# Two attention layers: low halves of late output-weight pieces moved on VectorE and ScalarE, one value projection moved between the first scores

## The chip, the cores and the metric

The kernel runs on one core of a Trainium2 chip. The metric is the device time of one execution in microseconds (us); the time quoted is the median of three runs. TensorE, VectorE, ScalarE, GpSimd and SyncE are written PE, DVE, ACT, POOL and SP, as in the rows of the profile. Each engine works through its own instructions in program order and waits on semaphores for the others.

## The reference, cut to what matters

Two blocks follow each other on x [1, 512, 1024], in float32. The first has two layers, each an attention, a layer norm with the residual, a mixture of 32 experts (two per token) and another layer norm. Its first attention is windowed with sinks, its second has low-rank (latent) queries, keys and values. The second block (convolutions, stick-breaking attention, retention, feed-forward) is not touched by the change.

```python
def swa_sink_gqa(x, w_in, sinks, w_o):      # layer 0
    ...
    m = jnp.maximum(jnp.max(sc, -1, keepdims=True), sink)
    e = jnp.exp(sc - m)
    p = e / (jnp.sum(e, -1, keepdims=True) + jnp.exp(sink - m))
    o = jnp.einsum('bnhgqk,bnkhd->bnqhgd', p.astype(vb.dtype), vb)
    return o.reshape(b, s, qd) @ w_o

def mla(x, w_down, q_norm, kv_norm, w_uq, w_ukv, w_o):   # layer 1
    ...
    kv = (ckv @ w_ukv).reshape(b, s, B_HEADS, B_NOPE + B_V)
    ...
    o = causal_attention(q, k, kv[..., B_NOPE:], (B_NOPE + B_ROPE) ** -0.5)
    return o.reshape(b, s, B_HEADS * B_V) @ w_o

for i in range(DEPTH):
    h = layer_norm(alpha * h + y, ...)       # y: the attention
    y = hier_moe(h, ...)
    h = layer_norm(alpha * h + y, ...)
```

## The kernel before, in words

The order of each engine's instructions is written out by hand, one Python function per engine (`_(pe)`, `_(act)`, `_(dve)`, `_(sp)`), in `window_layer` (first layer) and `latent_layer` (second).

**Split products.** A dense float32 product is three PE matmuls: both factors are split into a high part (ACT copies it to a rounded type) and a low part (DVE subtracts the high part), and `split_matmul` (L232 to L234) adds high by high, low by high and high by low. Weights come in pieces of 128x2048: SP loads a piece into one of two raw buffers (`load`), ACT makes the high part (`high(p)`, semaphore `hi_made`), DVE the low part (`low(p)`, `lo_made`). The output weight has four pieces, O to O+3. In `window_layer` these are pieces 6 to 9, written in the traces as win_w or win_w_o; in `latent_layer` pieces 8 to 11, written lat_w_o.

**Units.** The attention works on 16 units u, four heads by a tile n of 128 queries. For each unit PE makes `scores(u)`; DVE takes row maxima (`maxes(u)`: a reduction from PSUM and one to three tiny instructions); ACT takes exponentials (`exps(u)`); DVE divides (`norms(u)`: a reciprocal and four multiplications); PE transposes the probabilities (`turn(u)`); ACT copies them (`keep_turned(u)`); PE multiplies by the values (`mix(u)`); ACT and DVE make the high and low part of the result (`out_high(u)`, `out_low(u)`). Parts of the output projection (`out_part`) of a finished query tile stand between turn and mix of later units, so that PE has work while the other engines do the next softmax.

**First layer, where the change is.** Units 0, 2, 4 and 6 belong to query tile 0, so `out_part(0, 0)` comes with u = 7. PE's order there is mix(6), turn(7), scores(9), out_part(0,0), mix(7), turn(8), scores(10), out_part(0,1), mix(8). ACT's is exps(7), keep_turned(6), out_high(6), high(O+3), exps(8), keep_turned(7), out_high(7). DVE's is maxes(6), maxes(7), norms(6), out_low(5), maxes(8), low(O+2), norms(7), out_low(6), maxes(9), low(O+3), norms(8). The scores banks alternate, so scores(u) waits for exps(u-2). `out_part(0, 0)` needs pieces O and O+1, `out_part(0, 1)` needs O+2 and O+3.

**Second layer.** All scores share four banks: `scores(u)` waits for exps(u-1). Before scores(0) PE has made the value projections ("v", 0) and ("v", 1); the other six `up_unit(UP[("v", m)])` come two per unit, in PSUM bank 7 one after the other, each waiting for ACT's `keep_up` of the one before. ("v", 2) and ("v", 3) stood with u = 0, after turn(0). ACT's high(10) stood before out_high(2), high(11) before out_high(3); DVE's low(10) stood before norms(3), low(11) before norms(4). From u = 4 on out_part(0, ...) runs.

**After an attention.** SP loads expert weights into three sets. Those loads wait for points of the attention (`lo_made` complete, `scored`, `mixed`, `am.out_made`), later ones for blocks of experts that PE has used up. Routing and the experts follow, then the next layer.

Of the kernel before, what the change touches and what calls it, by code (L numbers as in the profile page):

```python
# [14 lines left out]
F32, BF16, I32, U32 = mybir.dt.float32, mybir.dt.bfloat16, mybir.dt.int32, mybir.dt.uint32  # L15
F32R = mybir.dt.float32r
ALU = mybir.AluOpType
# [548 lines left out]
def window_layer(k, base, layer, r, weights):  # L566
# [6 lines left out]
    raw = plan.put("raw", 80, [P, 2, 2048])  # L573
# [15 lines left out]
    K, V, Q, O = 0, 1, 2, 6  # L589
# [15 lines left out]
    with k.nc.Block(no_gpsimd_drain=True) as block:  # L605
# [380 lines left out]
        def _(dve):  # L986
# [6 lines left out]
            def low(p):  # L993
                dve.wait_ge(hi_made, p + 1)
                hi, lo = pieces[p]
                dve.tensor_tensor(laid(p, lo[:, :]), as_read(p), laid(p, hi[:, :].bitcast(F32)), ALU.subtract).then_inc(lo_made, 1)

            def rope(q):
                dve.wait_ge(bare_kept, q + 1)
                rope_tile(k, dve, link, bare[:, q % 2, :], k.ps[:, 6 if q < 2 else 3, :], tables, tmp, (rotated, q + 1))  # L1000
                dst = kT[:, q, :] if q < 2 else qT[:, q - 2, :]
                dve.tensor_tensor(dst, tmp[:, 0, :], tmp[:, 1, :], ALU.add).then_inc(placed, 1)
                dve.wait_ge(placed, q + 1)

            def maxes(u):
                n, gp, half = units[u]
                w, b = width(n), u % 2
                mine = sinks[:, 8 * gp:8 * gp + 8].rearrange("p (g a) -> p g a", g=2)[:, :, 2 * half:2 * half + 2]
                four = lambda y: y[:, b, :].rearrange("p (g i) -> p g i", g=2)
                dve.wait_ge(scored, u + 1)  # L1010
                link(dve.tensor_reduce(mx[:, b, :], heads(u)[:, :, 0:w], AX.X, ALU.max))
                link(dve.scalar_tensor_tensor(four(mx), four(mx), HD ** -0.5, mine, ALU.mult, ALU.max))
                link(dve.tensor_scalar(nm[:, b, :], mx[:, b, :], -1.0, None, ALU.mult))
                dve.tensor_tensor(four(es), mine, four(nm), ALU.add).then_inc(maxed, 1)
# [64 lines left out]
            norms(5)  # L1079
            out_low(4)  # L1080
            maxes(6)
            maxes(7)
            norms(6)
            out_low(5)
            maxes(8)
            low(O + 2)
            norms(7)
            out_low(6)
            maxes(9)
            low(O + 3)  # L1090
            for u in range(8, len(units)):
                norms(u)
                if u in (9, 11, 13, 15):
                    am.add(k, dve, (u - 9) // 4, (u - 9) // 2 % 2, 7)
                out_low(u - 1)
                if u + 2 < len(units):
                    maxes(u + 2)
                if u == 12:
                    am.norm(k, dve, 0)
# [307 lines left out]
def latent_layer(k, base, layer, cl, r, weights):  # L1407
# [80 lines left out]
    with k.nc.Block(no_gpsimd_drain=True) as block:  # L1488
# [64 lines left out]
        def _(pe):  # L1553
# [151 lines left out]
            for i in range(6, UP[("v", 2)]):  # L1705
                up_unit(i)
            scores(0)
            for u in range(len(units)):
                n, g = units[u]
                if u + 1 < len(units):  # L1710
                    scores(u + 1)
                turn(u, 0)
                if u < 3:
                    up_unit(UP[("v", 2 * u + 2)])
                if u >= 4:
                    out_part((u - 4) // 4, 2 * (u % 4))
                if n >= 2:
                    turn(u, 1)
                if u < 3:
                    up_unit(UP[("v", 2 * u + 3)])  # L1720
                if u >= 4:
                    out_part((u - 4) // 4, 2 * (u % 4) + 1)
                mix(u)
# [15 lines left out]
        def _(act):  # L1739
# [119 lines left out]
            for i in range(6, UP[("v", 2)]):  # L1859
# [3 lines left out]
                if i == 17:  # L1863
                    high(9)
            exps(0)
            for u in range(len(units)):
                keep_turned(u)
                if u < 3:
                    keep_up(UP[("v", 2 * u + 2)])
                if u + 1 < len(units):  # L1870
                    exps(u + 1)
                if u < 3:
                    keep_up(UP[("v", 2 * u + 3)])
                if u == 2:
                    high(10)
                if u == 3:
                    high(11)
                if u in (9, 13):
                    am.root(act, (u - 9) // 4)
                out_high(u)  # L1880
            copy = lambda dst, src: act.activation(dst, src, ACT.Copy)
            for half in range(2):
                take_turned(k, copy, act, rt, 0, half)
# [10 lines left out]
        def _(dve):  # L1894
# [106 lines left out]
            for u in range(len(units)):  # L2001
                if u + 1 < len(units):
                    maxes(u + 1)
                if u == 2:
                    low(10)
                if u == 3:
                    low(11)
                if u in (10, 14):
                    am.norm(k, dve, (u - 10) // 4)
                if u + 1 < len(units):  # L2010
                    norms(u + 1)
                if u >= 4 and u % 2 == 1:
                    am.add(k, dve, (u - 4) // 4, (u // 2) % 2, 7)
                out_low(u)
            am.norm(k, dve, 2)
            for half in range(2):
                am.add(k, dve, 3, half, out_bank(3, half))
# [1099 lines left out]
```

## Time and profile before

| what | value |
|---|---|
| median of 3 runs | 2742.12 us |
| lowest and highest | 2739.75, 2742.32 us |
| profiled execution, its own time | 2739.88 us |
| its span | 2738.1 us |
| mean granted clock of PE | 0.970 of full speed |
| PE busy | 2515.5 us, 92% of the span |
| DVE busy | 1074.0 us, 39% |
| ACT busy | 753.9 us, 28% |

Times in rows are counted from the span's start. The first attention takes the time up to about 232, its experts the time to about 720; the second attention ends at about 1015 and its experts at about 1500; the rest is the second block. A timeline row gives start, duration, engine, line, operation, output and inputs, shapes and count, and in brackets how long the engine was idle just before and what released it. PE matmuls are pipelined, so durations of neighbours overlap: starts are what to read.

### The profile page before, as it was taken

To read this page: it belongs to the slowest core of one execution; us is meant where nothing else is said; L and a number is where in the kernel's file an instruction comes from. 1 tells how busy PE (TensorE), PEld (TensorE's weight loads), DVE (VectorE), ACT (ScalarE), POOL (GpSimd) and SP (SyncE) were. 2 spreads that over 40 slices of the span, in tenths; PEclk is the share of its full clock that TensorE was granted. 3 is DMA by queue.
4 is the path that set the end of the run, shared out by engine and by line. 5 is a ranking of instruction groups with operands and counts; after the bars stand their busy time and mean duration, and the time that the engine had idled before them with its cause. 6 is when DMAs were issued, how large, how long until landed. Compare 5 with 4: busy or idle time off the path is not lost.

```text
span 2738.1 us, 36816 instructions
## 1 busy us (share of the span) xinstructions
PE 2515.5 (92%) x14582; PEld 1856.1 (68%) x14582; DVE 1074.0 (39%) x1594; ACT 753.9 (28%) x1217; POOL 182.2 (7%) x302
## 2 busy tenths in 40 slices
PE   8897999877898979998888899999999999999998
PEld 7575665444476666664544677888887877888887
DVE  4653111010354551110100666656542566556542
ACT  3530000000245420000001353543332354433331
POOL 0001111111000001111111000000000010000000
PEclk9998999999998989999999999999999999999999
DMA  6238999999722079999998412222333212223231
GB/s 169 69 139 352 406 407 406 411 406 406 282 93 78 9 297 402 404 406 411 409 411 350 173 62 93 77 93 93 107 124 108 70 62 93 78 93 108 93 123 54
DMA packets 174825, 576.56 MB, mean 211 GB/s; under 512 B 20496, under 2 KB 104016, under 8 KB 125042
## 3 DMA queue, kind: packets, MB, share of 16 engines
q1 hardware_dynamic: 164146, 558.07, 53.8%
q0 software_dynamic: 10560, 16.81, 1.9%
q8 instruction: 86, 1.41, 0.2%
q14 instruction: 33, 0.27, 0.0%
HBM read 569.56 MB, written 23.07 MB: 216 GB/s over the span
## 4 chain that ended last, share of the span: by engine, by line
PE 66%; SPq 20%; DMA 5%; DVE 4%; issue 3%; ACT 2%; POOLq 0%; DVEq 0%; POOL 0%; ACTq 0%
PE ps L232 15%; PE ps L233 15%; PE ps L234 15%; SPq L1151 13%; SPq L1157 7%; PE ps L1301 6%; PE ps L1319 4%; DMA first_weights<-in_moe_w_up 2%; PE ps L1271 1%; ACT lat_probs L1808 1%; PE ps L1634 1%; PE ps L1618 1%; PE ps L2300 1%; PE ps L2336 1%; DMA r_x<-resid 1%
## 5 line engine op out<-in xcount | busy, mean ns | idle before, releaser
L232 PE MATMUL ps<-l_h_hi,l_w_hi 128*128 128x512 f32 x896 | 353.0, 394 | 0.0
L1301 PE MATMUL ps<-first_weights,moe_xsT 128*64 128x256 f32 x2688 | 310.9, 381 | 44.5 <-DMA first_weights<-in_moe_w_up 28.0
L234 PE MATMUL ps<-l_h_hi,l_w_lo 128*128 128x512 f32 x896 | 348.8, 389 | 0.0
L233 PE MATMUL ps<-l_h_lo,l_w_hi 128*128 128x512 f32 x896 | 348.8, 389 | 0.0
L1380 DVE TENSOR_TENSOR moe_hid<-moe_silu,ps 128x256 f32<-128x256 f32 x64 | 27.0, 422 | 779.8 <-PE ps L1301 779.8
L1301 PEld LDWEIGHTS ps<-first_weights,moe_xsT 128*64 128x64 f32 x2688 | 224.1, 137 | 141.0 <-issue 90.7
L2830 DVE TENSOR_TENSOR l_w_lo<-l_raw,l_w_hi 128x2048 fp32r<-128x2048 f32 x76 | 174.1, 2293 | 270.2 <-ACT l_w_hi L2591 270.2
L1353 ACT ACTIVATE moe_ys<-ps 128x512 f32<-128x512 f32 x64 | 38.2, 597 | 685.7 <-PE ps L1319 685.7
L1319 PE MATMUL ps<-first_weights,moe_hidT 128*64 128x512 f32 x672 | 180.6, 685 | 38.5 <-DVE moe_hidT L1382 38.5
L2591 ACT ACTIVATE l_w_hi<-l_raw 128x2048 fp32r<-128x2048 f32 x76 | 145.6, 1918 | 179.5 <-PE ps L234 168.7
L232 PEld LDWEIGHTS ps<-l_h_hi,l_w_hi 128*128 128x128 f32 x896 | 168.2, 188 | 37.7 <-issue 2.9
L233 PEld LDWEIGHTS ps<-l_h_lo,l_w_hi 128*128 128x128 f32 x896 | 168.3, 188 | 35.5 <-issue 1.4
L234 PEld LDWEIGHTS ps<-l_h_hi,l_w_lo 128*128 128x128 f32 x896 | 168.2, 188 | 35.2
L1301 PE MATMUL ps<-first_ring,moe_xsT 128*64 128x256 f32 x1344 | 157.3, 384 | 25.5 <-DMA first_ring<-in_moe_w_up 14.8
L1301 PEld LDWEIGHTS ps<-first_ring,moe_xsT 128*64 128x64 f32 x1344 | 113.1, 138 | 72.8 <-issue 47.4
L1319 PEld LDWEIGHTS ps<-first_weights,moe_hidT 128*64 128x64 f32 x672 | 61.1, 154 | 129.1 <-issue 129.1
L1319 PE MATMUL ps<-first_ring,moe_hidT 128*64 128x512 f32 x352 | 88.8, 649 | 20.1 <-DVE moe_hidT L1382 20.1
L1259 POOL DMA_INDIRECT r_y<-moe_ys,moe_put x64 | 65.6, 1025 | 300.5 <-ACT moe_ys L1353 285.7
L1350 ACT ACTIVATE moe_silu<-ps 128x256 f32<-128x256 f32 x64 | 24.6, 384 | 215.7 <-PE ps L1301 215.7
L2873 DVE SCALAR_TENSOR_TENSOR l_gate<-l_glu,l_par,l_gate 128x512 f32<-128x512 f32 x120 | 81.8, 751 | 0.1
L232 PE MATMUL ps<-l_w_hi,l_act_hi 128*128 128x512 f32 x192 | 75.4, 393 | 0.0
L234 PE MATMUL ps<-l_w_hi,l_act_lo 128*128 128x512 f32 x192 | 75.0, 390 | 0.0
(577 smaller groups left out, 4314.6 us busy)
## 6 DMA issues: line engine op xcount, KB each, us to landing
first_weights<-in_moe_w_up SPq DMA_DIRECT2D x84, 1024.0 KB
first_weights<-in_moe_w_down SPq DMA_DIRECT2D x84, 1024.0 KB
first_weights<-in_moe_w_gate SPq DMA_DIRECT2D x84, 1024.0 KB
first_ring<-in_moe_w_up SPq DMA_DIRECT2D x44, 1024.0 KB
first_ring<-in_moe_w_down SPq DMA_DIRECT2D x44, 1024.0 KB
l_raw<-in_ffn_up SPq DMA_DIRECT2D x44, 1024.0 KB, 5.1
first_ring<-in_moe_w_gate SPq DMA_DIRECT2D x40, 1024.0 KB
l_raw<-in_w_in SPq DMA_DIRECT2D x22, 1024.0 KB, 5.1
```

The costliest lines, as they stand in the source:

```text
L232: pe.matmul(out, stationary[0], moving[0], start=first, stop=False)
L233: pe.matmul(out, stationary[0], moving[1], start=False, stop=False)
L234: return pe.matmul(out, stationary[1], moving[0], start=False, stop=last)
L1151: sp.dma_start(self.gate_up[s][m][:, 4 * c:4 * c + 4, :].rearrange("p j c -> p (j c)"), a[name][layer, e, c * 512:(c + 1) * 512, :].rearra ...
L1157: sp.dma_start(self.down[s][:, 2 * c:2 * c + 2, :].rearrange("p j c -> p (j c)"), a["moe_w_down"][layer, e, c * 256:(c + 1) * 256, :].rear ...
L1259: pool.indirect_dma_start(out=r.y_dram, out_offset=bass.IndirectOffsetOnAxis(ap=put[:, 0:1], axis=0), in_=ys[:, :], in_offset=None, bounds ...
L1301: ins = pe.matmul(k.ps[64 * h:64 * h + 64, 2 + m, 0:256], xsT[:, j, :], piece[:, j % 4, 256 * h:256 * h + 256], start=j == 0, stop=j == ND ...
L1319: ins = pe.matmul(k.ps[64 * h:64 * h + 64, 4, :], hidT[:, j % 2, 64 * (j // 2):64 * (j // 2) + 64], weights.down[s][:, j, 512 * h:512 * h ...
L1353: act.activation(ys[:, :], k.ps[:, 4, :], ACT.Copy).then_inc(ys_kept, 1)
L2591: act.activation(ring[n][0], piece(m), ACT.Copy).then_inc(hi_made, 1)
L2830: dve.tensor_tensor(lo, piece(m), hi.bitcast(F32), ALU.subtract).then_inc(lo_made, 1)
L2873: ins = dve.scalar_tensor_tensor(acc, glu[:, i, c:c + SEQ], par[:, l, 2, 2 * c + i:2 * c + i + 1], acc, ALU.mult, ALU.add)
```

## The change

In `window_layer` DVE makes the low parts of pieces O+2 and O+3 in two halves of 1024 columns each (`low_half`). The halves of O+2 stand before maxes(7) and before norms(7), and norms(7) now comes before maxes(8). The halves of O+3 stand before maxes(9) and behind norms(8). In `latent_layer` the value projection ("v", 2) moves on PE from behind turn(0) to between scores(0) and scores(1), and its copy on ACT to behind exps(0); high(10) and high(11) move behind out_high(2) and out_high(3), low(10) and low(11) from before norms(3) and norms(4) to behind out_low(2) and out_low(3).

```diff
@@ window_layer, DVE
+            def low_half(p, half):
+                dve.wait_ge(hi_made, p + 1)
+                hi, lo = pieces[p]
+                part = slice(1024 * half, 1024 * half + 1024)
+                return dve.tensor_tensor(lo[:, part], raw[:, p % 2, part], hi[:, part].bitcast(F32), ALU.subtract)
...
             out_low(4)
             maxes(6)
+            low_half(O + 2, 0)
             maxes(7)
             norms(6)
             out_low(5)
+            low_half(O + 2, 1).then_inc(lo_made, 1)
+            norms(7)
             maxes(8)
-            low(O + 2)
-            norms(7)
             out_low(6)
+            low_half(O + 3, 0)
             maxes(9)
-            low(O + 3)
             for u in range(8, len(units)):
                 norms(u)
+                if u == 8:
+                    low_half(O + 3, 1).then_inc(lo_made, 1)
...
@@ latent_layer, PE
             scores(0)
+            up_unit(UP[("v", 2)])
             for u in range(len(units)):
...
                 turn(u, 0)
-                if u < 3:
+                if 0 < u < 3:
                     up_unit(UP[("v", 2 * u + 2)])
@@ latent_layer, ACT
             exps(0)
+            keep_up(UP[("v", 2)])
             for u in range(len(units)):
                 keep_turned(u)
-                if u < 3:
+                if 0 < u < 3:
                     keep_up(UP[("v", 2 * u + 2)])
                 if u + 1 < len(units):
                     exps(u + 1)
                 if u < 3:
                     keep_up(UP[("v", 2 * u + 3)])
-                if u == 2:
-                    high(10)
-                if u == 3:
-                    high(11)
                 if u in (9, 13):
                     am.root(act, (u - 9) // 4)
                 out_high(u)
+                if u in (2, 3):
+                    high(8 + u)
@@ latent_layer, DVE
                 if u + 1 < len(units):
                     maxes(u + 1)
-                if u == 2:
-                    low(10)
-                if u == 3:
-                    low(11)
...
                     norms(u + 1)
...
                 out_low(u)
+                if u in (2, 3):
+                    low(8 + u)
```

**DVE in the first layer, from behind maxes(8) to norms(7), before.** The 128x2048 row is low(O+2); the three rows behind it are norms(7).

```order
L1013 TENSOR_SCALAR win_nm<-win_mx 128x4
L1014 TENSOR_TENSOR win_es<-win_sinks,win_nm 128x4
L996 TENSOR_TENSOR win_w_o_lo<-win_raw,win_w_o_hi 128x2048
L1019 TENSOR_TENSOR win_rd<-win_sm,win_es 128x4
L1020 RECIPROCAL win_rd<-win_rd 128x4
L1022 TENSOR_SCALAR win_probs<-win_probs,win_rd 128x256 x4
```

The same place now, from out_low(5) on. Lines are those of the changed file.

```order
L1034 TENSOR_TENSOR win_o_lo<-ps,win_o_hi 128x256
L1002 TENSOR_TENSOR win_w_o_lo<-win_raw,win_w_o_hi 128x1024
L1025 TENSOR_TENSOR win_rd<-win_sm,win_es 128x4
L1026 RECIPROCAL win_rd<-win_rd 128x4
L1028 TENSOR_SCALAR win_probs<-win_probs,win_rd 128x256 x4
L1017 TENSOR_REDUCE win_mx<-ps 128x4
L1018 SCALAR_TENSOR_TENSOR win_mx<-win_mx,win_sinks 128x4
L1019 TENSOR_SCALAR win_nm<-win_mx 128x4
L1020 TENSOR_TENSOR win_es<-win_sinks,win_nm 128x4
```

Only half a piece stands ahead of norms(7) now, and maxes(8), with its reduction L1017, has moved behind norms(7).

**DVE in the second layer, u = 2, before.** The first two rows are maxes(3), the 128x2048 row is low(10), then come norms(3), out_low(2) and the reduction of maxes(4).

```order
L1944 TENSOR_REDUCE lat_nm<-ps 128x4
L1945 TENSOR_SCALAR lat_nm<-lat_nm 128x4
L1912 TENSOR_TENSOR lat_w_o_lo<-lat_raw,lat_w_o_hi 128x2048
L1950 RECIPROCAL lat_rd<-lat_sm 128x4
L1952 TENSOR_SCALAR lat_probs<-lat_probs,lat_rd 128x128 x4
L1959 TENSOR_TENSOR lat_o_lo<-ps,lat_o_hi 128x2x128
L1944 TENSOR_REDUCE lat_nm<-ps 128x4
```

And now:

```order
L1953 TENSOR_REDUCE lat_nm<-ps 128x4
L1954 TENSOR_SCALAR lat_nm<-lat_nm 128x4
L1959 RECIPROCAL lat_rd<-lat_sm 128x4
L1961 TENSOR_SCALAR lat_probs<-lat_probs,lat_rd 128x128 x4
L1968 TENSOR_TENSOR lat_o_lo<-ps,lat_o_hi 128x2x128
L1921 TENSOR_TENSOR lat_w_o_lo<-lat_raw,lat_w_o_hi 128x2048
L1953 TENSOR_REDUCE lat_nm<-ps 128x4
```

low(10) has left its place ahead of norms(3) for one directly ahead of maxes(4).

**PE in the second layer, from scores(0) to turn(0), now.** The first three rows are scores(0), the six L232 to L234 rows are ("v", 2), then come scores(1) and turn(0).

```order
L1627 MATMUL ps<-lat_k,lat_q 128x128 x4
L1630 MATMUL ps<-lat_kr,lat_qr 128x128 x4
L1632 MATMUL ps<-maskab,identb 128x128 x4
L232 MATMUL ps<-lat_uv_hi,lat_c_kv_hi 128x512
L233 MATMUL ps<-lat_uv_lo,lat_c_kv_hi 128x512
L234 MATMUL ps<-lat_uv_hi,lat_c_kv_lo 128x512
L232 MATMUL ps<-lat_uv_hi,lat_c_kv_hi 128x512
L233 MATMUL ps<-lat_uv_lo,lat_c_kv_hi 128x512
L234 MATMUL ps<-lat_uv_hi,lat_c_kv_lo 128x512
L1627 MATMUL ps<-lat_k,lat_q 128x128 x4
L1630 MATMUL ps<-lat_kr,lat_qr 128x128 x4
L1632 MATMUL ps<-maskab,identb 128x128 x4
```

Before, scores(1) followed scores(0) directly, and the six projection matmuls stood behind turn(0).

## Rows read from the trace of the kernel before

**Rows 1.** The page: chain that ended last, shares of the span by engine.
```profile
PE 66%; SPq 20%; DMA 5%; DVE 4%; issue 3%; ACT 2%; POOLq 0%; DVEq 0%; POOL 0%; ACTq 0%
```
**Rows 2.** Waits of PE, 106 to 137 us: us in total, times, longest.
```profile
PE ps L747 <- DVE win_probs L1022: 7.6, 4, 4.7
```
**Rows 3.** Timeline of PE, first layer: start, us, instructions [idle before, releaser].
```profile
118.58 0.65 PE L759 MATMUL ps<-win_probsT,win_v 128*64 128x256 f32 x4 [0.19 <-ACT win_probsT L907]
123.98 1.97 PE L747 MATMUL ps<-cst,win_probs 128*128 128x128 f32 x8 [4.75 <-DVE win_probs L1022]
...
128.73 0.50 PE L232 MATMUL ps<-win_w_hi,win_o_hi 128*128 128x512 f32 x1
...
131.70 1.08 PE L759 MATMUL ps<-win_probsT,win_v 128*64 128x256 f32 x8
134.40 1.09 PE L747 MATMUL ps<-cst,win_probs 128*128 128x128 f32 x8 [1.61 <-DVE win_probs L1022]
...
136.91 0.50 PE L232 MATMUL ps<-win_w_o_hi,win_o_hi 128*128 128x512 f32 x1
```
**Rows 4.** Timeline of DVE, same stretch.
```profile
113.17 1.23 DVE L1011 TENSOR_REDUCE win_mx<-ps 128x4 f32<-128x1024 f32 x1 [1.16 <-PE ps L734]
...
118.44 1.23 DVE L1011 TENSOR_REDUCE win_mx<-ps 128x4 f32<-128x1024 f32 x1 [1.86 <-PE ps L734]
...
120.18 2.29 DVE L996 TENSOR_TENSOR win_w_o_lo<-win_raw,win_w_o_hi 128x2048 fp32r<-128x2048 f32 x1
...
122.79 1.14 DVE L1022 TENSOR_SCALAR win_probs<-win_probs,win_rd 128x256 f32<-128x256 f32 x4
...
130.59 2.28 DVE L996 TENSOR_TENSOR win_w_lo<-win_raw,win_w_hi 128x2048 fp32r<-128x2048 f32 x1
```
**Rows 5.** Timeline of ACT, same stretch: end of exps(7), and high(O+3).
```profile
117.82 0.22 ACT L898 ACTIVATION_READ_ACCUMULATOR win_probs<-ps,win_nm 128x1 f32 x1
...
119.56 1.90 ACT L879 ACTIVATE win_w_hi<-win_raw 128x2048 fp32r<-128x2048 f32 x1
```
**Rows 6.** Instructions on win_raw: duration ns min/median/max, first and last start.
```profile
L1034 DVE TENSOR_TENSOR win_w_lo<-win_raw,win_w_hi x1: 1216/1216/1216, 11.1 to 11.1; 128x1024 fp32r<-128x1024 f32 x1
```
**Rows 7.** Windows: PE, PEld, DVE, ACT, POOL busy (count), PE clock, DMA share, GB/s.
```profile
119.20:124.00 4.80, 0.05 (x3) 0.02 (x1) 4.63 (x12) 4.10 (x11) 0.00 (x0) 0.77 0.00 0
124.00:128.70 4.70, 4.70 (x18) 3.02 (x18) 0.26 (x1) 1.02 (x1) 0.00 (x0) 0.50 0.02 3
```
**Rows 8.** Timeline of PE, second layer: the first row of scores or turn.
```profile
833.92 0.71 PE L1618 MATMUL ps<-lat_k,lat_q 64*128 64x128 f32 x8 [0.78 <-ACT lat_v L1800]
...
837.92 0.71 PE L1618 MATMUL ps<-lat_k,lat_q 64*128 64x128 f32 x8 [2.53 <-ACT lat_probs L1808]
...
845.65 0.71 PE L1618 MATMUL ps<-lat_k,lat_q 64*128 64x128 f32 x8
...
863.26 1.12 PE L1634 MATMUL ps<-cst,lat_probs 128*128 128x128 f32 x4 [3.19 <-DVE lat_probs L1952]
...
866.90 2.08 PE L1618 MATMUL ps<-lat_k,lat_q 64*128 64x256 f32 x8 [0.71 <-ACT lat_probs L1808]
...
872.29 1.97 PE L1634 MATMUL ps<-cst,lat_probs 128*128 128x128 f32 x8 [1.61 <-DVE lat_probs L1952]
```
**Rows 9.** Timeline of ACT, second layer: high(10).
```profile
857.99 1.90 ACT L1763 ACTIVATE lat_w_o_hi<-lat_raw 128x2048 fp32r<-128x2048 f32 x1
```
**Rows 10.** Timeline of DVE, second layer: the reduction of maxes(4).
```profile
863.46 1.22 DVE L1944 TENSOR_REDUCE lat_nm<-ps 128x4 f32<-128x1024 f32 x1
```
**Rows 11.** Windows of the second layer, columns as in rows 7.
```profile
837.90:842.10 4.20, 4.18 (x28) 3.54 (x29) 1.92 (x7) 0.60 (x1) 0.00 (x0) 0.59 0.00 0
...
875.80:878.90 3.10, 3.10 (x25) 2.28 (x23) 1.32 (x5) 1.34 (x6) 0.00 (x0) 0.94 0.62 262
```
**Rows 12.** Timeline of SP: first expert weights behind the last output part, first layer.
```profile
209.59 0.80 SPq L1151 DMA_DIRECT2D first_ring<-in_moe_w_gate  x2
```
**Rows 13.** A window of the first experts, columns as in rows 7.
```profile
300.00:400.00 100.00, 93.62 (x666) 61.02 (x662) 10.11 (x21) 7.25 (x15) 16.68 (x28) 0.95 1.02 406
```

## The prediction

> **What bounds the kernel now.** I read the chain of work that ended last first: PE holds 66% of it and the DMA queue of SP 20% [rows 1]. So there are two kinds of stretches: the attentions and the second block, where PE sets the pace, and the experts, where the weight stream does: 406 GB/s with the DMA engines full, while PE waits in between [rows 13]. The edits lie in the attentions only. The second view is PE's waits there: between 106 and 137 us PE waits 7.6 us for normalised probabilities, 4.7 of them at one place [rows 2]. The third is the timeline of PE, DVE and ACT around such a wait, to see what stood ahead of the late work. The fourth is the granted clock of the same stretches.
>
> **First layer, what is late.** mix(6) starts at 118.58 and lasts 0.65, then PE has nothing until turn(7) at 123.98 [rows 3]. turn(7) needs norms(7), which ends at 122.79 + 1.14 = 123.93 [rows 4]. Its input, exps(7), was done at 118.04 [rows 5]. Between the two DVE did maxes(8), 118.44 to 120.26, and then the whole of low(O+2), 2.29 us [rows 4]. The gap is not all: PE is granted 0.50 (1.2 GHz) from 124.0 to 128.7, straight behind it, though it works without a pause there, and 0.77 over the gap itself [rows 7].
>
> **First layer, step by step.** A half piece costs 1.22 us (a row of this very form exists) against 2.29 for the whole [rows 4, 6], so each split adds 2 x 1.22 - 2.29 = 0.15 us to DVE. The first half of O+2 lies in the idle 1.16 us before maxes(7), the second in the idle 1.86 us before maxes(8) [rows 4]; cost on the path 0.05 at most. If that cover were gone each would cost its 1.22. norms(7) takes 1.55 us (122.38 to 123.93). It now starts at 118.1 and ends at 119.65, so turn(7) starts at 119.7. turn and scores of a wide unit take 136.91 - 134.40 = 2.51 us at full clock: out_part(0,0) starts at 122.2. What it needs is there: maxes(8) now 119.6 to 121.4, out_low(6) to 121.7. out_part takes 131.70 - 128.73 = 2.97: mix(7) starts at 125.2, takes about 1.0 to the next start, turn(8) could start at 126.2. Does norms(8) come in time? high(O+3) ends at 121.46 [rows 5], so the first half of O+3 runs 121.7 to 122.9, maxes(9) to 124.6, norms(8) to 126.15. That is a tie. The second half of O+3 ends at 127.3, and out_part(0,1), its only reader, starts at 126.2 + 2.5 = 128.7. Before, low(O+3), from 130.59, held norms(8) and turn(8) until 134.40 [rows 3, 4]. **The term is 134.40 - 126.2 = 8.2 us.** Its ends: if a half piece does come in front of norms(8), 7.0; with the tie won, 8.4. I take 8.2, the sum of rows. It holds only with the clock at full speed, which I expect since the gap that came before the fall shrinks from 4.75 to 0.5 us.
>
> The Trainium skill, page "VectorE: DVE Perf Modes", section on the TRN2 errata, speaks against the halves: operands in SBUF pay a fixed extra latency in every instruction, so work should not be cut small. The trace agrees, at 0.15 us per cut; by that rule alone the change would cost 0.3 us on an engine that idles beside it.
>
> **Second layer, first scores.** scores(0) starts at 833.92 and scores(1) at 837.92, since scores, maxes, exps and the next scores form one chain of 4.0 us in which PE idles 2.53 [rows 8]. ("v", 2) is six matmuls of some 0.39 us or less; it fits in the idle time, and ACT's copy of it comes behind exps(0), where ACT would wait for turn(0). Then the same chain of 4.0 us links scores(1) and scores(2), plus 0.1 for keep_turned(0) ahead of exps(1): scores(2) at 842.0 against 845.65 [rows 8]. PE's own work in that time (turn(0), ("v", 3), mix(0)) just fits. **This term is 3.65 us.** It includes that the granted clock, 0.59 between 837.9 and 842.1 [rows 11], stays up, because the idle before it shrinks from 2.53 to about 1. If it does not, the term is 3.1. Units 1 and 2 keep their pace, which ACT's copies set.
>
> **Second layer, pieces 10 and 11.** I count in times of before, to be shifted by 3.65. scores(4) ends at 863.26 - 3.19 = 860.07; turn(3) then waited 3.19 us for norms(3), which stood behind low(10) [rows 8]. Now norms(3) is done by 858.3 and turn(3) and mix(3) run at once. What is late next: out_high(2) goes first on ACT, high(10) runs 858.4 to 860.3 instead of from 857.99 [rows 9], low(10) with its 2.29 to 862.6, and behind it is maxes(4), which starts at 862.6 instead of 863.46 [rows 10]. From maxes(4) to scores(5) it is 866.90 - 863.46 = 3.44. So scores(5) starts at 866.05, only 0.85 earlier: the wait for norms(3) has largely become one, of about 4.2 us, for maxes(4). From scores(5) to turn(4) it was 5.39 with 1.61 of waiting for norms(4), behind low(11). low(11) now runs behind out_low(3), so 5.39 - 1.61 = 3.78: turn(4) at 869.83 against 872.29, 2.46 earlier. Then the clock: PE now works without a pause from 866.05. In the first layer it was back at full speed after 4.7 us of that [rows 7], which would be 870.8 here; before, it came back near 875.8, and the part between turn(4) and mix(4) ran slow [rows 11]. That gives about 1.1 more. **This term is 3.6 us.** Ends: 2.46 if all stays at half clock as before; 5.0 if the clock never falls, where maxes(5), behind low(11), becomes the limit. I take the value between, by the row of the first layer.
>
> The Trainium skill, page "TensorE: Matmul & The Clock Gate", section on HAM oscillation, says that gaps between groups of matmuls put the array back to 1.2 GHz, so that a gap costs more than itself. That speaks against the new 4.2 us gap. By it the 5.0 us end of the last term is out of reach and the rest of the sum stands; the trace agrees [rows 8, 11], with 0.59 behind an idle of 2.53 us.
>
> **Does it reach the end?** After both places PE has no other long wait, and every transfer of expert weights waits for a point of the attention: the six of the first ring are issued at 209.59, behind the last output part [rows 12]. The stream at 406 GB/s starts from there and moves with it, unless it has a start that the attention doesn't set. I charge nothing for it.
>
> **The sum.** 8.2 + 3.65 + 3.6 = 15.45. The profiled execution took 2739.88 us for a span of 2738.1: 2724.4 for it. It is 2.2 us below the median of the runs, 2742.12, from which it is 2726.7. I predict **2726 us**.
>
> **Rivals.**
> (a) One gain is lost: the tie at norms(8) and the order behind it fail, or the gap at scores(5) grows and eats the second layer's terms. For it: both margins are under 0.2 us. Against: then other work moves earlier too. Time 2742.1 less 8.2 or less 7.3: 2734 to 2735, and anything between there and the forecast.
> (b) The expert stage swallows the gains: it is bound by its weight stream [rows 13], and if the stream's start were not tied to the attention, PE would only wait longer for weights. For it: SP's 20% of the chain. Against: the issue at 209.59. Time 2742.
> (c) Slower. The new gap of 4.2 us at scores(5) drops the clock, and it stays at 1.2 GHz through the dense part behind, where each us of work takes two. The sum has it back at full speed by 870.8. To lose the 15.4 us and 5.5 more, at half a us lost for each us run slowly, the slow stretch would have to go on for another 42 us, to about 913; from there on this case decides. For it: the gap is longer than any before it in this layer. Against: 4.7 us of steady work brought the clock back in the first layer. Time then 2748.
> (d) That the halves don't do what they say is excluded: the order of DVE shows them.
>
> **The chances.** A difference of 0.2%, 5.5 us, is about what a measurement of this kernel can tell from none. Forecast 0.77; (a) 0.14, still faster; (b) 0.06; (c) 0.03. So faster 0.91, same 0.06, slower 0.03. Bounds of the terms: 7.0 + 3.1 + 2.5 = 12.6 and 8.4 + 3.7 + 5.0 = 17.1, from either of 2739.9 and 2742.1: 2722.8 to 2729.5. With run-to-run spread and the nearer half of (a) the range is 2721 to 2732.
>
> **What would show it.** In the changed profile: turn(7) of the first layer with idle of 0.5 us or less before it, clock 1.00 from 120 to 129, out_part(0,1) near 128.7; in the second layer the 2.53 us idle before scores(1) down to about 1, and one idle of about 4.2 us before scores(5) with 1.2 GHz behind it for some 5 us. The experts must take as long as before, 8 us earlier in the first layer and 15 in the second. The prediction is wrong if norms(8) comes later than mix(7), or if the experts' stretch grows by what the attention gave.

## The result and the profile after

| what | before | changed |
|---|---|---|
| median of 5 runs on one chip | 2739.79 us | 2721.77 us |
| lowest and highest | 2737.54, 2742.32 us | 2719.08, 2726.82 us |
| profiled execution, its own time | 2739.88 us | 2721.77 us |
| its span | 2738.1 us | 2719.9 us |
| mean granted clock of PE | 0.970 | 0.976 |
| PE busy | 2515.5 us, 92% | 2500.8 us, 92% |

The ratio is 0.9931, 95% interval 0.9919 to 0.9942: 16 to 22 us faster. Run again beside the experiments, the same kernel gave 0.9941 (0.9928 to 0.9955). The forecast was 2726 us, with a gain of 15.45 us.

The first view is the chain of work that ended last, which answers to [rows 1]. Its shares add up to only 45% of the span: this time the chain goes back no further than 1493 us, the end of the second experts, so it doesn't tell how much the experts' weight stream holds.

```profile
PE 41%; DVE 2%; ACT 1%; DMA 1%; issue 0%; SPq 0%; DVEq 0%; ACTq 0%
```

The second is the list of PE's waits from 98 to 130 us, which now takes in turn(5) to turn(8), as [rows 2] did up to 137. The columns are the sum in us, the number of waits and the longest.

```profile
PE ps L747 <- DVE win_probs L1028: 3.1, 3, 2.1
```

7.6 us of waiting for normalised probabilities have become 3.1, and the longest, 4.7, is 2.1. The timeline of PE in the first layer answers to [rows 3]: start, duration, instructions, and in brackets the idle time before.

```profile
110.36 1.70 PE L747 MATMUL ps<-cst,win_probs 128*128 128x128 f32 x8 [0.73 <-DVE win_probs L1028]
...
117.70 1.11 PE L747 MATMUL ps<-cst,win_probs 128*128 128x128 f32 x4 [2.11 <-DVE win_probs L1028]
...
121.89 1.09 PE L747 MATMUL ps<-cst,win_probs 128*128 128x128 f32 x8
...
128.69 1.09 PE L747 MATMUL ps<-cst,win_probs 128*128 128x128 f32 x8 [0.26 <-DVE win_probs L1028]
...
131.21 0.50 PE L232 MATMUL ps<-win_w_o_hi,win_o_hi 128*128 128x512 f32 x1
```

These are turn(5), turn(6), turn(7), turn(8) and out_part(0,1). The 4.75 us before turn(7) are gone altogether, but turn(8) comes at 128.69, not at 126.2, and there is a wait of 2.11 before turn(6), a place that the change doesn't touch. The windows of the same stretch, with the columns of [rows 7], show what is different:

```profile
110.00:114.50 4.50, 4.14 (x18) 2.75 (x18) 2.87 (x8) 2.51 (x10) 0.00 (x0) 0.62 0.49 203
117.70:121.30 3.60, 3.60 (x14) 2.18 (x14) 2.81 (x8) 1.41 (x5) 0.00 (x0) 0.55 0.00 0
121.30:128.70 7.40, 7.14 (x45) 4.58 (x43) 6.37 (x17) 5.23 (x13) 0.00 (x0) 1.00 0.02 3
```

The granted clock fell to its lower level near 111 us, made turn(6) late, and fell again behind that wait. The profile of before had full speed up to 114.5 at least. The experiments come back to this.

The second layer, PE's timeline, answers to [rows 8]: scores(0), scores(1), scores(2), scores(4), turn(3), mix(3), scores(5), turn(4), scores(6).

```profile
825.46 0.72 PE L1627 MATMUL ps<-lat_k,lat_q 64*128 64x128 f32 x8 [0.78 <-ACT lat_v L1810]
829.46 0.71 PE L1627 MATMUL ps<-lat_k,lat_q 64*128 64x128 f32 x8 [1.08 <-ACT lat_probs L1818]
833.46 0.71 PE L1627 MATMUL ps<-lat_k,lat_q 64*128 64x128 f32 x8
...
845.81 1.13 PE L1627 MATMUL ps<-lat_k,lat_q 64*128 64x256 f32 x8
...
847.76 0.60 PE L1643 MATMUL ps<-cst,lat_probs 128*128 128x128 f32 x4
...
849.05 0.66 PE L1657 MATMUL ps<-lat_probsT,lat_v 128*64 128x128 f32 x8 [0.69 <-ACT lat_probsT L1828]
853.79 2.08 PE L1627 MATMUL ps<-lat_k,lat_q 64*128 64x256 f32 x8 [4.08 <-ACT lat_probs L1818]
...
857.36 1.46 PE L1643 MATMUL ps<-cst,lat_probs 128*128 128x128 f32 x8
...
862.52 1.14 PE L1627 MATMUL ps<-lat_k,lat_q 64*128 64x256 f32 x8
```

scores(0) to scores(2) takes 8.00 us, before 11.73. turn(3) doesn't wait for norms(3) any more, and the new wait stands before scores(5). The row names ACT's exponentials as what released it, but they waited for maxes(4), which stood on DVE directly behind low(10):

```profile
848.14 2.29 DVE L1921 TENSOR_TENSOR lat_w_o_lo<-lat_raw,lat_w_o_hi 128x2048 fp32r<-128x2048 f32 x1 [1.37 <-ACT lat_w_o_hi L1773]
850.35 1.22 DVE L1953 TENSOR_REDUCE lat_nm<-ps 128x4 f32<-128x1024 f32 x1
```

The clock behind that wait, in windows:

```profile
849.70:853.80 4.10, 0.02 (x3) 0.01 (x2) 2.07 (x4) 1.99 (x9) 0.00 (x0) 0.71 0.14 46
853.80:858.50 4.70, 4.70 (x27) 3.23 (x28) 4.28 (x8) 2.01 (x2) 0.00 (x0) 0.53 0.00 0
858.50:862.50 4.00, 4.00 (x31) 3.08 (x29) 1.67 (x6) 2.85 (x9) 0.00 (x0) 1.00 0.85 283
```

PE works without a pause from 853.8, at 1.2 GHz for most of the next 4.7 us, and then at full speed. In the profile of before the lower clock held from 863 until about 876.2, 9.3 us behind its scores(5): the window up to 875.8 is at 0.50 and the next, 3.1 us long, at 0.94 [rows 11].

The first expert weights, which answer to [rows 12], are issued 7.3 us earlier than before, and a window of the experts is as before, as [rows 13]:

```profile
202.30 0.80 SPq L1160 DMA_DIRECT2D first_ring<-in_moe_w_gate  x2
```

```profile
300.00:400.00 100.00, 93.39 (x654) 60.33 (x652) 10.11 (x21) 7.46 (x15) 16.85 (x30) 0.95 1.02 403
```

**Where the 18.2 us between the two profiles come from.** Differences of start times, one after the other:

| stretch | earlier by, us |
|---|---|
| first layer, up to turn(8) | 5.7 |
| from there to the issue of the expert weights | 1.6 |
| first experts, and up to scores(0) | 1.2 |
| scores(0) to scores(2) | 3.7 |
| scores(4) to scores(6) | 4.2 |
| from there to the end of the second attention | 1.5 |
| second experts | -1.9 |
| second block | 2.2 |

The three places of the change give 5.5, 3.7 and 4.2 us (the first counted from turn(4), where the two profiles stand 0.17 apart). The rest comes from places where both run the same code. Two of these are visible in the clock: the profile of before has a fall near 169 and one near 968, and the changed one has none at the matching places. First the window near 169 of before:

```profile
168.90:173.00 4.10, 4.10 (x18) 2.39 (x18) 1.56 (x3) 1.34 (x3) 0.00 (x0) 0.59 0.92 318
```

And of the changed kernel:

```profile
163.20:167.30 4.10, 4.09 (x25) 3.03 (x26) 2.95 (x5) 1.33 (x3) 0.00 (x0) 1.00 0.97 338
```

Near 968 the granted clock is 0.64 from 967.2 to 972.0 in before, and 1.00 from 950.8 to 955.6 in the changed kernel. The two falls lie in the stretches of 1.6 and 1.5 us of the table. Near 169 the price can be read: from turn(13) to turn(14) it is 8.08 us with the fall and 6.47 without. Whether the change has a part in that one is taken up with the second run of before.

### The profile page after: what moved, and what is told of

Its sections match the earlier page's. It is cut to its first block and busy times, and to the rows that moved or that the text cites. A ratio compares the mean times of both kernels' runs of the same rounds, so it can differ in the third digit from the quotient of the medians.

```text
span 2719.9 us, 36818 instructions
## 1 busy us (share of the span) xinstructions
PE 2500.8 (92%) x14582; PEld 1849.2 (68%) x14582; DVE 1074.3 (39%) x1596; ACT 753.2 (28%) x1217; POOL 181.6 (7%) x302
## 5 line engine op out<-in xcount | busy, mean ns | idle before, releaser
L232 PE MATMUL ps<-l_h_hi,l_w_hi 128*128 128x512 f32 x896 | 353.4, 394 | 0.0
L234 PE MATMUL ps<-l_h_hi,l_w_lo 128*128 128x512 f32 x896 | 349.2, 390 | 0.0
L1328 PE MATMUL ps<-first_weights,moe_hidT 128*64 128x512 f32 x672 | 172.1, 658 | 38.7 <-DVE moe_hidT L1391 38.7
L232 PEld LDWEIGHTS ps<-l_h_hi,l_w_hi 128*128 128x128 f32 x896 | 168.3, 188 | 37.3 <-issue 2.9
L234 PEld LDWEIGHTS ps<-l_h_hi,l_w_lo 128*128 128x128 f32 x896 | 168.2, 188 | 35.3
L1328 PEld LDWEIGHTS ps<-first_ring,moe_hidT 128*64 128x64 f32 x352 | 31.2, 152 | 66.1 <-issue 66.1
L232 PE MATMUL ps<-l_w_hi,l_act_hi 128*128 128x512 f32 x192 | 75.4, 393 | 0.0
```

Of the source, the lines that this page charges most:

```text
L232: pe.matmul(out, stationary[0], moving[0], start=first, stop=False)
L234: return pe.matmul(out, stationary[1], moving[0], start=False, stop=last)
L1328: ins = pe.matmul(k.ps[64 * h:64 * h + 64, 4, :], hidT[:, j % 2, 64 * (j // 2):64 * (j // 2) + 64], weights.down[s][:, j, 512 * h:512 * h ...
```

## The experiments

**Each part alone.** Three kernels, each with one of the three parts of the change in the kernel before, and the changed kernel again, all beside runs of before on one chip.

The first has only the edits of `window_layer`:

```diff
...
+            low_half(O + 2, 0)
...
+            low_half(O + 2, 1).then_inc(lo_made, 1)
+            norms(7)
             maxes(8)
-            low(O + 2)
-            norms(7)
             out_low(6)
+            low_half(O + 3, 0)
             maxes(9)
-            low(O + 3)
...
+                if u == 8:
+                    low_half(O + 3, 1).then_inc(lo_made, 1)
```

(`low_half` itself is added as in the change.)

> Only the edits of the first layer; the second layer as before. Theory S (the schedule decides, and the clock's falls are its own in each execution): turn(8) of the first layer starts 5.5 to 8.5 us earlier than the 134.40 of before, 8.2 if PE's clock is 1.00 from 106 to 121, some 2.5 less if it falls there as it did in the changed kernel's profile (0.59 from 110 to 114); the time is 2732 to 2734, ratio 0.997 to 0.998. Theory C (the clock follows the schedule): the fall at 110.9 us and the 2.11 us wait for norms(6) come again exactly as in the changed kernel's profile, turn(8) at 128.7, and no fall near 169 us. In both the stretch of the second layer from scores(0) to scores(6) takes 45.0 us as before.

Measured: 2729.97 us, ratio 0.996 (0.9946 to 0.9973), 11 us faster. PE's timeline, turn(7) and turn(8):

```profile
119.63 1.09 PE L747 MATMUL ps<-cst,win_probs 128*128 128x128 f32 x8 [0.45 <-DVE win_probs L1028]
...
126.11 1.09 PE L747 MATMUL ps<-cst,win_probs 128*128 128x128 f32 x8
```

These are the times that the prediction gave, 119.7 and 126.2, and in this profile the clock did not fall near 111, as in before's. From turn(4) to turn(8) it is 20.48 us where before took 28.73: the term of 8.2 us. The total gained more than was expected, 11 us against 7 to 8; in the profile, 1.6 us of that come from the clock near 169, which did not fall here.

The second has only the value projection moved:

```diff
             scores(0)
+            up_unit(UP[("v", 2)])
...
-                if u < 3:
+                if 0 < u < 3:
                     up_unit(UP[("v", 2 * u + 2)])
...
             exps(0)
+            keep_up(UP[("v", 2)])
...
-                if u < 3:
+                if 0 < u < 3:
                     keep_up(UP[("v", 2 * u + 2)])
```

> Only the value projection moved. Theory S: from scores(0) to scores(2) of the second layer 8.0 us in place of 11.73, so 3.7 us gained, and all behind it as before: the wait for norms(3) of 3.2 us and the one for norms(4) of 1.6 come back. Time 3.7 us less, ratio 0.9987. Rival (the freed time is waited for again at norms(3) or scores(5), since the low parts are what is late): scores(6) starts less than 2 us earlier against scores(0) and the ratio is 1.000.

Measured: 2736.6 us, ratio 0.9989 (0.998 to 0.9998), 3 us faster. scores(0), scores(1) and scores(2) on PE:

```profile
831.19 0.71 PE L1618 MATMUL ps<-lat_k,lat_q 64*128 64x128 f32 x8 [0.78 <-ACT lat_v L1801]
835.19 0.72 PE L1618 MATMUL ps<-lat_k,lat_q 64*128 64x128 f32 x8 [1.08 <-ACT lat_probs L1809]
839.20 0.71 PE L1618 MATMUL ps<-lat_k,lat_q 64*128 64x128 f32 x8
```

8.01 us for the two steps, against 11.73: 3.7 us. The waits for norms(3) and norms(4) are back, 3.18 and 1.60 us. From scores(4) to scores(6) it is 20.54 us, where before took 20.94: turn(3) still ran at full speed here (0.66 us for four matmuls against 1.12), and the clock fell only behind it.

The third has only pieces 10 and 11 moved:

```diff
-                if u == 2:
-                    high(10)
-                if u == 3:
-                    high(11)
...
                 out_high(u)
+                if u in (2, 3):
+                    high(8 + u)
...
-                if u == 2:
-                    low(10)
-                if u == 3:
-                    low(11)
...
                 out_low(u)
+                if u in (2, 3):
+                    low(8 + u)
```

> Only high(10), high(11), low(10) and low(11) moved. Theory S: scores(2) as before (11.73 us behind scores(0)); from scores(4) to scores(6), 20.94 us in before and 16.71 in the changed kernel's profile, 16.7 to 18.5, with one wait of about 4 us for exps(4) in place of the waits of 3.2, 0.7 and 1.6. Ratio 0.998 to 0.9995. Rival (the halved clock eats it, since the longest single wait grows from 3.2 to 4.1 us): more than 19 us for that stretch.

Measured: 2735.35 us, ratio 0.9978 (0.9968 to 0.9987), 6 us faster. PE's timeline, scores(4), scores(5) and scores(6):

```profile
856.38 1.14 PE L1618 MATMUL ps<-lat_k,lat_q 64*128 64x256 f32 x8
...
864.37 1.82 PE L1618 MATMUL ps<-lat_k,lat_q 64*128 64x256 f32 x8 [4.09 <-ACT lat_probs L1808]
...
872.62 0.70 PE L1618 MATMUL ps<-lat_k,lat_q 64*128 64x256 f32 x4
```

The wait for maxes(4) is there, 4.09 us, and scores(6) still comes 16.24 us behind scores(4), where before took 20.94: 4.7 us. That is a little better than the 16.7 to 18.5 expected. The halved clock did not eat the gain, so the rival is out.

The fourth is the changed kernel itself, with no edit.

> The changed kernel once more. Theory S: the first layer's turn(8) between 126 and 129 us, the granted clock falling at other places than in the first profile of it: either no fall at 110.9 us, or one of the falls near 165 and 952 us that the first profile lacked. Theory C: the same falls within 1 us, turn(8) at 128.7, transitions at the same places. Time 2717 to 2727 in both.

Measured: 2723.02 us, ratio 0.9941 (0.9928 to 0.9955). The three parts give 11, 3 and 6 us, together 20, where the whole gives 16 (this run) to 19 (the first): additive within their intervals. The three stretches themselves, in the profiles of the three parts, give 8.2, 3.7 and 4.7, together 16.6. Its profile is the one that shows the forecast's first layer, since here too the clock did not fall near 111. PE's timeline, mix(6), turn(7), mix(7), turn(8) and out_part(0,1):

```profile
118.51 0.65 PE L759 MATMUL ps<-win_probsT,win_v 128*64 128x256 f32 x4 [0.19 <-ACT win_probsT L907]
119.61 1.09 PE L747 MATMUL ps<-cst,win_probs 128*128 128x128 f32 x8 [0.45 <-DVE win_probs L1028]
...
125.07 1.08 PE L759 MATMUL ps<-win_probsT,win_v 128*64 128x256 f32 x8
126.09 1.10 PE L747 MATMUL ps<-cst,win_probs 128*128 128x128 f32 x8
...
128.61 0.50 PE L232 MATMUL ps<-win_w_o_hi,win_o_hi 128*128 128x512 f32 x1
```

and its window:

```profile
118.50:128.70 10.20, 9.74 (x61) 6.37 (x61) 8.63 (x22) 7.60 (x23) 0.00 (x0) 1.00 0.08 14
```

**Before again**, one execution with a profile, to see whether the clock's fall near 111 belongs to the change.

> The kernel before, once more. If the falls of the granted clock belong to each execution and not to the code, its profile may differ from the first one: with or without a fall near 111 (turn(6) at 116.2 or 117.5 us) and near 169 us, and turn(8) between 134.0 and 135.6. The experts' two stretches take 510 to 515 us with some us of difference to the first profile.

Measured: 2741.83 us. turn(5), turn(6), turn(7) and turn(8):

```profile
110.10 1.97 PE L747 MATMUL ps<-cst,win_probs 128*128 128x128 f32 x8 [0.73 <-DVE win_probs L1022]
...
117.35 0.66 PE L747 MATMUL ps<-cst,win_probs 128*128 128x128 f32 x4 [2.10 <-DVE win_probs L1022]
...
125.09 1.97 PE L747 MATMUL ps<-cst,win_probs 128*128 128x128 f32 x8 [5.00 <-DVE win_probs L1022]
...
135.51 0.66 PE L747 MATMUL ps<-cst,win_probs 128*128 128x128 f32 x4 [1.38 <-DVE win_probs L1022]
```

The fall doesn't belong to the change: here it is without it. The window that holds it, of this execution and then of the first profile of before, same kernel and same work:

```profile
109.00:114.50 5.50, 4.77 (x30) 3.18 (x28) 2.69 (x10) 2.51 (x10) 0.00 (x0) 0.69 0.59 191
```

```profile
109.00:114.50 5.50, 3.39 (x28) 2.23 (x26) 4.13 (x13) 2.56 (x11) 0.00 (x0) 1.00 0.50 191
```

The fall stands in 6 of the 10 profiles of this study, four of kernels with the edits of `window_layer` and two without. So the length from turn(4) to turn(8) has to be compared like with like:

| us, turn(4) to turn(8) | no fall near 111 | fall near 111 |
|---|---|---|
| old order | 28.73, 28.59 | 30.27, 30.36 |
| new order | 20.48, 20.50 | 23.19, 21.33 |

Without the fall the change gives 8.1 to 8.3 us, with it 7.1 to 9.0. The first pair of profiles crossed the table, 28.73 to 23.19, which is why it showed 5.5.

The fall near 169 is another matter. Before turn(13) PE waits 2.04 or 2.05 us in all ten profiles. In three of the four with the old order the clock falls there, and turn(14) comes 8.04 to 8.15 us behind turn(13); in none of the six with the new order does it fall, and the step takes 6.47 to 6.49. Ten profiles don't settle whether that is chance. If it isn't, about 1.6 us more are a gain of the first layer's edits, which no term of the prediction has.

**Are the halves needed, or only the order?** The changed kernel with whole pieces at the new places:

```diff
-            low_half(O + 2, 0)
             maxes(7)
...
-            low_half(O + 2, 1).then_inc(lo_made, 1)
+            low(O + 2)
             norms(7)
...
-            low_half(O + 3, 0)
             maxes(9)
...
                 if u == 8:
-                    low_half(O + 3, 1).then_inc(lo_made, 1)
+                    low(O + 3)
```

> The changed kernel, but the low parts of O+2 and O+3 are made whole: O+2 ahead of norms(7), O+3 behind norms(8); norms(7) still comes before maxes(8). Theory O (the gain of the first layer comes from the order, the cut itself is worth little): turn(7) near 120.4 and turn(8) near 126.9 us in place of 119.6 and 126.1, so 0.8 us lost of 8.3; ratio 0.994 to 0.995. Rival H (the halves carry it): the whole piece of 2.29 us ahead of norms(7) comes back on the path in full, turn(8) at 128.4 or later. Read at a granted clock of 1.00; a fall near 111 us adds some 1.5 to 2.6 to both.

Measured: 2723.55 us, ratio 0.9924 (0.991 to 0.9937), not to be told from the changed kernel's, and not slower, as the expected 0.994 to 0.995 would have it. The whole low(O+2) on DVE, and then turn(7) and turn(8) on PE:

```profile
117.80 2.28 DVE L996 TENSOR_TENSOR win_w_o_lo<-win_raw,win_w_o_hi 128x2048 fp32r<-128x2048 f32 x1
```

```profile
121.60 1.09 PE L747 MATMUL ps<-cst,win_probs 128*128 128x128 f32 x8 [1.25 <-DVE win_probs L1028]
...
128.08 1.09 PE L747 MATMUL ps<-cst,win_probs 128*128 128x128 f32 x8
```

turn(7) waits 1.25 us, and 22.67 us from turn(4) to turn(8) lies between the two of the table. So most of the gain comes from norms(7) ahead of maxes(8) and low(O+3) behind norms(8), which were not tried apart from each other.

What the halves add is too little for the times of the runs, but the profiles show it. This one had the clock's fall near 111 and was back at full speed before turn(6). The profile with halves that had the same course is that of the experiment on the wait before scores(5), further down, whose first layer is that of the changed kernel. From turn(6) to turn(7), whole piece first, then halves:

```profile
117.61:121.60 3.99, 2.74 (x18) 1.47 (x19) 3.92 (x9) 2.50 (x7) 0.00 (x0) 1.00 0.00 0
```

```profile
115.86:118.79 2.93, 2.73 (x19) 1.47 (x19) 2.86 (x9) 1.45 (x6) 0.00 (x0) 1.00 0.00 0
```

The work of PE is the same and the clock is 1.00 in both; the difference is PE's wait for norms(7), 1.25 against 0.19 us, and it is the length by which a whole piece exceeds a half, 2.28 - 1.22. At turn(8) 1.0 us of it is left (10.47 against 9.47 us behind turn(6)). The expectation had 0.8. The Trainium skill, page "VectorE: DVE Perf Modes", section on the TRN2 errata, says that an instruction on SBUF operands pays its latency anew each time. The trace agrees: two halves of 1.22 against one whole of 2.28, 0.16 us for each cut, less than the 1.0 us that they give here.

**The tie at norms(8).** One line moved in the changed kernel:

```diff
             for u in range(8, len(units)):
+                if u == 8:
+                    low_half(O + 3, 1).then_inc(lo_made, 1)
                 norms(u)
-                if u == 8:
-                    low_half(O + 3, 1).then_inc(lo_made, 1)
```

> The changed kernel, with the second half of O+3 directly ahead of norms(8) in place of behind it. If norms(8) is the tie that the prediction says, turn(8) comes 1.2 us later, 127.3 at full clock against 126.1, with 1.2 us or so of idle before it. If PE has slack there (something else sets turn(8)), it stays at 126.1 to 126.5. No sure difference in the time.

Measured, in one execution: 2720.14 us, and on PE turn(8) at

```profile
126.83 1.09 PE L747 MATMUL ps<-cst,win_probs 128*128 128x128 f32 x8 [1.13 <-DVE win_probs L1028]
```

A half piece in front of norms(8) becomes 1.13 us of idle time before turn(8), nearly its whole 1.22, and from turn(7) to turn(8) it takes 7.68 us, where the other profiles with the clock at full speed there have 6.48 to 6.54. The prediction's tie was real: DVE had less than 0.1 us of slack there. The total of a single execution says nothing about one us.

**The wait before scores(5).** If low(10) stands behind maxes(4) instead of in front of it, it lies beside ACT's exponentials:

```diff
                 if u + 1 < len(units):
                     maxes(u + 1)
+                if u in (3, 4):
+                    low(7 + u)
...
                 out_low(u)
-                if u in (2, 3):
-                    low(8 + u)
```

> The changed kernel, but in the second layer low(10) and low(11) stand behind maxes(4) and maxes(5), ahead of norms(4) and norms(5). If the 4.1 us wait before scores(5) is there because maxes(4) stands behind low(10), it shrinks to 1.5 or so, and the clock doesn't fall behind it: from scores(4) to scores(6) 12.3 to 13 us against 16.6, and 4 us less in time, ratio to before 0.991 to 0.993. Rival (ACT's high(10) and exps(4) set scores(5), not DVE's order): the stretch stays above 15.5 us.

Measured: 2719.33 us (2716.08 to 2721.74), ratio 0.9916 (0.9902 to 0.9929). PE's timeline, scores(4), scores(5) and scores(6):

```profile
843.78 1.13 PE L1627 MATMUL ps<-lat_k,lat_q 64*128 64x256 f32 x8
...
849.38 2.08 PE L1627 MATMUL ps<-lat_k,lat_q 64*128 64x256 f32 x8 [1.70 <-ACT lat_probs L1818]
...
859.01 1.13 PE L1627 MATMUL ps<-lat_k,lat_q 64*128 64x256 f32 x8
```

The wait is 1.70 us instead of 4.08, and scores(5) comes 5.60 us behind scores(4), not 7.98. But from scores(4) to scores(6) it takes 15.23 us, only 1.5 less than the changed kernel's 16.71. Of the expectation the half on the order came true (maxes(4) behind low(10) was what the wait was for) and the half on the clock did not. The windows of the wait and of what follows show why:

```profile
847.70:849.40 1.70, 0.02 (x2) 0.03 (x2) 1.70 (x1) 1.70 (x9) 0.00 (x0) 0.84 0.22 77
849.40:854.90 5.50, 5.50 (x29) 4.03 (x30) 3.39 (x10) 2.00 (x2) 0.00 (x0) 0.50 0.00 0
```

The clock fell inside the wait of 1.7 us, which has 0.84, and stayed at 1.2 GHz for the 5.5 us behind it; behind the wait of 4.1 us it was 0.53 over 4.7. Shortening the wait took away most of its idle time and not the fall of the clock, and the step from scores(5) to scores(6) took 9.63 us, where it was 8.73. The median is the lowest of all kernels run, 2.4 us under the changed one, but the intervals of the two ratios overlap, so that it is better than the changed kernel isn't shown. The ratio lies within the one expected, but that doesn't bear out the expected 4 us: the stretch gave 1.5 of them.

## Where the prediction failed, and where it held

The direction and the three mechanisms held, and three steps of the working failed. The first is "it holds only with the clock at full speed, which I expect": in the changed kernel's own profile the granted clock fell near 111 us and again at 117.7, turn(8) came at 128.69 instead of 126.2, and the stretch from turn(4) to turn(8) gave 5.5 us in place of 8.2. turn(8) also waited 0.26 us for norms(8) there, which is the prediction's own sign of being wrong; the second profile of the same kernel, without the falls, has no such wait. The second is the term of pieces 10 and 11: 3.6 us, measured at 4.0 to 4.7 in five profiles. The third is "I charge nothing for it": 4.8 us of the profiled pair's 18.2 came from places that run the same code, 1.6 of them from the clock near 169. The gain of 18.0 us is 2.6 above the sum; the second step accounts for 0.4 to 1.1 of that, the clock near 169 for 1.6 if it is the change's doing, and the rest stays open.

- **The sign of the change** was right and its size came out larger: 18.0 us by medians of five where the sum gave 15.45. That the profiled pair, at 18.2, lies above the sum too is in part luck. In this pair the three places gave only 13.4, since the clock near 111 took 2.7 from the first layer's term, and 4.8 us came from places that run the same code; only the 1.6 of them near 169 may be a gain of the change. The sum lies just outside the first interval (16 to 22 us) and inside the second run's (12 to 20).
- **The base.** 2726 was rounded from 2724.4, against the profiled execution, and 2726.7, against the median of three runs of before. The median of five runs is 2739.79, from which the sum gives 2724.3. 1.7 of the 4.2 us between 2726 and 2721.77 are this choice.
- **First layer, 8.2 us:** right in its size and in its steps where the clock stays at full speed. turn(7), out_part(0,0), mix(7), turn(8) and out_part(0,1) stand within 0.2 us of what was worked out, in both profiles of the new order without that fall. That norms(8) ties with mix(7) was shown by the half piece in front of it.
- **Second layer, 3.65 us:** right, 3.7 in all six profiles that have the edit. The idle before scores(1) is 1.08 us. The condition on the clock held too: in the four profiles with 2.52 or 2.53 us of idle there the clock fell behind it, each time for some 3.4 us, and in the six with 1.08 it stayed at 1.00.
- **Pieces 10 and 11, 3.6 us: the term that was mis-sized.** It measured 4.0 to 4.7 in five profiles. The step "turn(4) at 869.83 against 872.29, 2.46 earlier" gave 2.77, since the wait before scores(5) was 4.08 and not 4.2 and turn(4) followed 3.57 us behind and not 3.78. The step "that gives about 1.1 more", for the clock, gave 1.5. Its size was a slip of reading: by [rows 11] the clock of before was back at about 876.2, not 875.8, and half of the 3.9 us from turn(4) to there, less half of the 1.0 us from 869.83 to 870.8, is 1.5. The new wait and what is late in it, maxes(4) behind low(10), were right.
- **"It holds only with the clock at full speed, which I expect":** this step failed as it was put. In the changed kernel's own profile turn(7) has no idle time before it, but the clock is 1.00 only from 121.3 on, 0.55 before that, and turn(8) comes 2.5 us later than forecast. The clock had fallen at 111, at a place that the change doesn't touch, and it fell there in a run of before as well. I had read one profile of before as the state of the clock, where it is one of at least two that the same code can have.
- **Reaching the end, nothing charged:** right within what the experts vary. The length of the second experts' stretch, from the last `r_x<-resid` transfer before it to the first `open_rows` load behind it, is 510.2 to 514.2 us over ten profiles with the same code in it, and the two profiles of the result differ there by 1.9 us against the change.
- **The rivals.** (a), a gain lost, and (b), the experts swallowing it, didn't come: each part alone reached the end. (c), the clock staying down behind the new wait, stopped after 4.7 us. By the Trainium skill, page "TensorE: Matmul & The Clock Gate", section on HAM oscillation, a gap between groups of matmuls returns the array to 1.2 GHz. The traces agree at this place, with 0.53 behind 4.08 us in the changed kernel and 0.50 behind 1.70 us in the last experiment; elsewhere a gap of 2.04 us did so in three profiles of ten.

What stays open: what decides between the two courses of the clock near 111, whether the change has a part in the clock near 169, and how much of the first layer's gain each of its two moves would bring alone.

## What to carry to other kernels

Look at what stands on a helping engine between the input of a late instruction and that instruction: putting norms(7) ahead of maxes(8), and a weight split behind norms(8), gave most of the first layer's 8.2 us, and cutting the splits in two about 1.0 of them. Before a stretch of two profiles is compared, compare its granted clock just ahead of the change; if that differs, take more profiles until there is a pair that agrees. When a wait is shortened, charge the work behind it at the lower clock as well, until a profile shows that it ran at the higher.

## What the runs showed of the hardware

- **The same instructions got two different courses of the clock.** Up to turn(5) before, the changed kernel and all others have the same idles on PE, 0.69, 1.15 and 0.73 or 0.74 us, and yet the granted clock fell near 111 us in 6 of 10 executions and stayed at full speed in 4. In the six with the fall turn(5) started at 108.9 to 110.4 us, in the four without at 110.3 to 110.5: when the stretch begins may be what decides, but no run here shows it. The fall cost 1.5 to 1.8 us in the old order and 0.8 to 2.7 in the new. The Trainium skill, page "TensorE: Matmul & The Clock Gate", section "What's actually happening", says that the number of slow matmuls at a kernel's start varies from run to run. Here the course of the clock varied from one execution to the next in the middle of a kernel, in two executions each of before and of the changed kernel.
- **Short waits are enough for a fall, and don't always bring one.** The clock fell within 1.70 us of idle time, and near 111 behind idles of 1.15 us at most. The wait of 2.11 us before turn(6) was followed by a fall in the changed kernel's first profile (0.55) and by full speed in the ones of pieces 10 and 11 alone and of the whole pieces.
- **The experts' stream isn't constant to the microsecond.** With the same code the first experts took 512.9 to 516.3 us (from the issue that [rows 12] shows to the first load of the next layer) and the second 510.2 to 514.2, as large a spread as one term of this prediction.
